# A streaming-encoder step on one core: front pieces spread over the expert half blocks in other proportions, and attention scores issued ahead of the turn

## The reference

```
z   = RMSNorm(x) @ w_in                  # q, k, v of two attentions, forget logits, gates
p   = softmax(q_m k_m / 8 + bias), m=0,1;  a = (p_0 - lam p_1) @ v        # 8 heads, diff attention
ob  = softmax(q k / 8 + C[t] - C[s]) @ v                                 # 8 heads, FoX
x   = x + (sig(gA) * (norm(oa) @ w_pa) + sig(gB) * (ob @ w_pb)) @ w_o
q   = xb @ wq (xb = RMSNorm(x));  sc = q . subkeys;  top 16 of each half, top 16 of the sums
x   = x + sum over 8 heads x 16 experts of  g * gelu(u_e . xb) * v_e      # rows u_e, v_e gathered
y   = RMSNorm_final(x)
```

## Time and profile before

| | before |
|---|---|
| time, median of 3 runs (lowest to highest) | 2603.12 us (2593.22 to 2603.57) |
| the profiled execution: its time / its span | 2613.62 us / 2611.8 us |
| PE busy | 2156.7 us, 83% of the span |
| DVE busy | 1436.7 us, 55% |
| ACT busy | 524.9 us, 20% |
| mean DMA rate | 293 GB/s |
| mean granted PE clock | 0.867 of full |

### The profile page before, as it was taken

One profiled execution on the slowest core, in us unless ns is written; L12 is line 12 of the kernel. 1 busy time (PEld: TensorE's weight loads), 2 busy tenths in 40 slices (PEclk: granted clock), 3 DMA queues, 4 the chain that ended last, 5 costly groups with the idle time before them and its releaser, 6 DMA issues. The chain is left out here.

```text
span 2611.8 us, 23600 instructions
## 1 busy us (share of the span) xinstructions
PE 2156.7 (83%) x7844; PEld 1226.7 (47%) x7844; DVE 1436.7 (55%) x3495; ACT 524.9 (20%) x1354; POOL 693.0 (27%) x697
## 2 busy tenths in 40 slices
PE   7989989989488986887997778989875998998775
PEld 6845566556245642344663234466321434664321
DVE  0021113666355369667559865554894656337956
ACT  2321101111152111343110134301111432011111
POOL 0000000244122123233233522332443223123433
PEclk9988899999679997898998877899887777778778
DMA  8832355698768896788999966699989558888887
GB/s 250 280 106 71 123 190 181 243 394 302 300 236 310 338 350 256 295 309 328 404 405 368 354 258 237 244 402 403 415 323 389 214 222 303 329 305 323 320 324 313
DMA packets 139305, 765.05 MB, mean 293 GB/s; under 512 B 18608, under 2 KB 42464, under 8 KB 52016
## 3 DMA queue, kind: packets, MB, share of 16 engines
q0 software_dynamic: 78336, 570.46, 56.1%
q1 hardware_dynamic: 24912, 154.73, 16.2%
q10 hardware_dynamic: 35936, 38.35, 4.4%
HBM read 744.77 MB, written 18.30 MB: 292 GB/s over the span
## 5 line engine op out<-in xcount | busy, mean ns | idle before, releaser
L1187 PE MATMUL acc<-ring,diag 128*128 128x512 f32 (+1 forms) x1720 | 947.8, 704 | 244.6 <-DVE diag L1521 237.0
L597 POOL DMA_INDIRECT ring<-in_uv,stage x544 | 634.8, 1167 | 1386.8 <-issue 843.2
L1510 DVE CUSTOM_DVE_ANT_0 ring<-ring,xb 128x1024 f32<-128x1024 f32 x544 | 649.5, 1220 | 139.3 <-DMA ring<-in_uv,stage 129.0
L1187 PEld LDWEIGHTS acc<-ring,diag 128*128 128x128 f32 (+1 forms) x1720 | 361.5, 221 | 751.6 <-issue 425.3
L869 ACT ACTIVATE gel<-dots 128x1 f32<-128x1 f32 x544 | 105.5, 201 | 1001.8 <-DVE dots L1510 983.7
L1521 DVE TENSOR_SCALAR diag<-ident,gel,gw 128x128 f32<-128x128 f32 x406 | 141.5, 357 | 216.3 <-ACT gel L869 204.3
L967 PE MATMUL pz<-F,wbuf 128*128 128x416 f32 (+1 forms) x656 | 242.8, 530 | 3.6 <-issue 1.4
L615 POOL COPY stage<-idx 128x4 int32<-128x4 int32 x136 | 55.4, 408 | 508.0 <-DVE gw L1466 488.7
L967 PEld LDWEIGHTS pz<-F,wbuf 128*128 128x128 f32 (+1 forms) x656 | 126.7, 196 | 113.1 <-issue 113.1
L1366 DVE TENSOR_REDUCE nmax<-ps 128x1 f32<-128x128 f32 (+4 forms) x72 | 35.6, 495 | 241.3 <-PE ps L1026 83.7
L1535 DVE SCALAR_TENSOR_TENSOR vsum<-ring,coefd,vsum 128x1024 f32<-128x1024 f32 x109 | 140.7, 1291 | 4.5 <-DVE coefd L1528 0.7
(11 more groups left out here) (267 smaller groups left out, 1997.6 us busy)
## 6 DMA issues: line engine op xcount, KB each, us to landing
wbuf<-in_w_z SPq DMA_DIRECT2D x52, 1024.0 KB, 5.4
wbuf<-in_w_q SPq DMA_DIRECT2D x40, 1024.0 KB, 8.1
wbuf<-in_w_pa SPq DMA_DIRECT2D x20, 1024.0 KB, 7.5
wbuf<-in_w_o SPq DMA_DIRECT2D x20, 1024.0 KB, 7.8
wbuf<-in_w_pb SPq DMA_DIRECT2D x20, 512.0 KB, 6.8
ring<-in_uv,stage POOLq DMA_INDIRECT x544, 8.4
zT<-F ACTq DMA_DIRECT2D x28, 208.0 KB, 2.9
wbuf<-in_w_sk SPq DMA_DIRECT2D x5, 1024.0 KB, 7.0
```

Of the source, the lines that this page charges most:

```text
L597: pool.indirect_dma_start(out=ring[:, slot, :], out_offset=None, in_=d["uv"], in_offset=bass.IndirectOffsetOnAxis(ap=stage[:, a, k:k + 1], ...
L1187: last = nc.tensor.matmul(acc[0:nq, c * 512:(c + 1) * 512], diag[:, parity, 0:nq], ring[:, slot, D + c * 512:D + (c + 1) * 512], start=Fal ...
L1510: nc.vector.tensor_tensor_reduce(out=u, in0=u, in1=xb[:, t % 2, :], scale=1.0, scalar=0.0, op0=ALU.mult, op1=ALU.add, accum_out=dots[:, sl ...
```

## The change

It has three parts. The prices in `weight_of` are others, so the same pieces fall behind other half blocks. The scores of a head are issued one step earlier on PE (for fronts 0 to 3; front 4 keeps its step, but the scores come ahead of the turn), and on ACT and DVE the exponential and the maximum of head s come ahead of the copy and the merge of head s-1. Front 0 gets four score banks, the two halves of `acc` being the third and fourth, and the projections of every front rotate over four banks.

```
-    if what == "project":
-        return 12.0
+    if what == "project":
+        return 1.4
     if p == 0:
-        return 12.0 if i == TILES - 1 else 4.0
+        return 3.0 if i == TILES - 1 else 0.5
     if ATTEND <= p < NORM_O:
-        return 5.0
+        return 1.8
     if p >= TOP:
-        return 6.0
+        return 1.8
+    if YPROJ <= p < OPROJ:
+        return 0.7
     if OPROJ <= p < NORM_X or QPROJ <= p < SCORE:
-        return 1.8
-    return 4.0 if p in (NORM_O, TURN_O, NORM_X, TURN_X) else 3.5
+        return 0.45
+    return 0.5
...
+        def banks(t):
+            return ps + ([acc[:, 0:512], acc[:, 512:1024]] if t == 0 else pz)
...
         def score_banks(t):
-            return 4 if 0 < t < TILES - 1 else 2
+            return 4 if t < TILES - 1 else 2
...
+                ahead = score_banks(t) == 4
+                if step_ == 0 and ahead:
+                    for v in STEPS[0]:
+                        for n in score_tasks(v):
+                            scores(n)
+                coming = step_ + ahead
+                for v in STEPS[coming] if coming < len(STEPS) else []:
+                    for n in score_tasks(v):
+                        scores(n)
                 before = STEPS[step_ - 1] if 1 <= step_ <= len(STEPS) else []
-                now = STEPS[step_] if step_ < len(STEPS) else []
-                for i in range(max(len(before), len(now))):
-                    if i < len(before):
-                        turn(before[i])
-                    if i < len(now):
-                        for n in score_tasks(now[i]):
-                            scores(n)
-                    if i < len(before):
-                        pv(before[i], i == 1)
+                for i in range(len(before)):
+                    turn(before[i])
+                    pv(before[i], i == 1)
...
-                        if f >= 2:
-                            pe.wait_ge(pq_stored, PC * t + f - 1)
+                        if f >= 4:
+                            pe.wait_ge(pq_stored, PC * t + f - 3)
                         for k in range(8):
-                            last = nc.tensor.matmul(ps[f % 2][:, 0:nq], w[:, k, j * P:(j + 1) * P],
+                            last = nc.tensor.matmul(banks(t)[f % 4][:, 0:nq], w[:, k, j * P:(j + 1) * P],
```

More of the change, by code:

```diff
@@ L768, in attend @@
                 nq, nk = rows_of(t), keys_of(t)
+                for v in STEPS[s] if s < len(STEPS) else ():
+                    for n in score_tasks(v):
+                        act.wait_ge(maxed, 24 * t + n + 1)
+                        if n >= 4:
+                            m = n - 4
+                            act.wait_ge(turned, 16 * t + (m // 2 if m < 16 else m - 8) + 1)
+                        nc.scalar.activation(fa(t).prob[0:nq, n % 4, 0:nk], score_bank(t, n)[0:nq, 0:nk], ACT.Exp,
+                                             bias=nmax[0:nq, n:n + 1], accum_out=rsum[0:nq, n:n + 1]
+                                             ).then_inc(exped, 1)
                 for u in STEPS[s - 1] if 1 <= s <= len(STEPS) else ():
@@ L844, in front @@
                         act.wait_ge(pq_mm, PC * t + f + 1)
-                        nc.scalar.activation(fa(t).pqT[:, f, 0:nq], ps[f % 2][:, 0:nq], ACT.Copy).then_inc(pq_stored, 1)
+                        nc.scalar.activation(fa(t).pqT[:, f, 0:nq], banks(t)[f % 4][:, 0:nq], ACT.Copy).then_inc(pq_stored, 1)
                 elif p == SCORE:
@@ L849, in front @@
                         nc.scalar.activation(fa(t).sc[0:nq, 4 * q:4 * q + 4, :],
-                                             ps[q % 2][0:nq, 0:512].rearrange("p (k q) -> p k q", k=4), ACT.Copy
+                                             banks(t)[q][0:nq, 0:512].rearrange("p (k q) -> p k q", k=4), ACT.Copy
                                              ).then_inc(sc_stored, 1)
@@ L1114, in front @@
                         for k in range(4):
-                            last = nc.tensor.matmul(ps[f % 2][:, P:P + nq], wb[:, k, j * P:(j + 1) * P],
+                            last = nc.tensor.matmul(banks(t)[f % 4][:, P:P + nq], wb[:, k, j * P:(j + 1) * P],
                                                     fa(t).obT[:, k, 0:nq], start=(k == 0), stop=(k == 3))
@@ L1342, in attend @@
                     open_attention(t)
+                for v in STEPS[s] if s < len(STEPS) else ():
+                    for n in score_tasks(v):
+                        dve.wait_ge(scored, 24 * t + n + 1)
+                        nc.vector.tensor_reduce(nmax[0:nq, n:n + 1], score_bank(t, n)[0:nq, 0:nk], AX.X, ALU.max,
+                                                negate=True).then_inc(maxed, 1)
                 for u in STEPS[s - 1] if 1 <= s <= len(STEPS) else ():
@@ L1375, in merge @@
                     dve.wait_ge(y_mm, 8 * t + f + 1)
-                    step(nc.vector.tensor_tensor(fa(t).mT[:, f, 0:nq], ps[f % 2][:, 0:nq], fa(t).gates[:, f, 0:nq], ALU.mult))
-                    step(nc.vector.tensor_tensor(fa(t).ybg[:, 0:nq], ps[f % 2][:, P:P + nq], fa(t).gates[:, 8 + f, 0:nq],
+                    step(nc.vector.tensor_tensor(fa(t).mT[:, f, 0:nq], banks(t)[f % 4][:, 0:nq], fa(t).gates[:, f, 0:nq], ALU.mult))
+                    step(nc.vector.tensor_tensor(fa(t).ybg[:, 0:nq], banks(t)[f % 4][:, P:P + nq], fa(t).gates[:, 8 + f, 0:nq],
                                                  ALU.mult))
@@ L1386, in add_x @@
                 cc = slice(c * CW, (c + 1) * CW)
-                nc.vector.tensor_tensor(x2[0:nq, cc], ps[c % 2][0:nq, 0:CW], fa(t).xres[0:nq, cc], ALU.add
+                nc.vector.tensor_tensor(x2[0:nq, cc], banks(t)[c][0:nq, 0:CW], fa(t).xres[0:nq, cc], ALU.add
                                         ).then_inc(x2_stored, 1)
```

33 lines of the change are left out of this document (9 added, 24 removed).

## The result

The changed kernel takes 2656.88 us (median of 4 runs, 2645.55 to 2665.97), the kernel before 2601.65 us on the same chip (4 runs). The ratio is 1.0217, with a 95% interval of 1.0169 to 1.0264: **some 55 us slower**, where 31 us faster was forecast, and outside the range.

A forecast was written before the change was run, and what follows sets the result against it. Beside attention nothing was full, PE and DVE taking turns; beside projections PE and DMAs were full, beside the search DVE. Terms -8 + 4 - 9.5 - 12 - 5, say -31, gave 2583 us profiled, 2572 us median; range 2518 to 2614.

The forecast's parts named there:

- Front 0, -8: Front 0, ahead of the experts: 10.5 us of merge waits go, 4 us of copy waits come, free banks save 2.
- Tile 0, +4: Tile 0: chunks -10, attention +8, projections -6 and search +12 us, in sum 4 us longer.
- 135 against 126.9: Tile 0's attention: 21 half blocks instead of 13 take 135 us, 112 of DVE work and 23 of idle time.
- Tile 1, -9.5: Tile 1: attention +1.5, norm -4 and projections -7 us, in sum 9.5 us shorter.
- tile 2, -12: Tile 2: attention -1 us at clock 0.87, the rest as in tile 1, in sum 12 us shorter.
- I take 0.96: Tile 1's attention: PE's clock rises from 0.88 to 0.96 as most idle pieces go, giving 159.5 us.
- The first step also stands directly behind the load … I add 4: Tile 1's attention: the first step, directly behind the load of the queries, adds 4 us of idle time.
- Tile 3, -5: Tile 3: front 4's attention +6 us and its projections -11 us, in sum 5 us shorter.
- Projections ... -11: Tile 3, front 4's projections: ten half blocks instead of 14 at the same clock 0.73 save 11 us.
- (B): Rival: filled gaps bring the clock back in attention, up to -85 us, 2518 to 2555 us; chance 0.22.
- (D): Rival: 26 moved half blocks cost their transfer beside attention, as adds held back delay gathers; +24, 2627 us; chance 0.12.
- (E): Rival: a drain at each table load delays ACT's copy by 1.4 us, giving 2642 us; chance 0.03.

The follow-up runs named there:

- order_only: The changed kernel with the old prices, keeping the new order and banks: 2589.74 us, ratio 0.9973 to the kernel before.
- load_apart: The changed kernel with the load of the queries of fronts 1 to 3 priced 2.0 instead of 0.5: 2624.57 us, ratio 1.0120.
- load_23: The changed kernel with the load of the queries priced 2.0 instead of 0.5 for fronts 2 and 3 only: 2615.48 us, ratio 1.0066.
- chunks_back: order_only with new prices for front 1 alone (load 2.0), tile 0's chunks standing where they were before: 2593.51 us, ratio 0.9971.
- wide_order: front4_old with front 4's y and query projections 128 columns wide instead of 32: 2538.51 us, ratio 0.9764.
- wide_234: wide_order with the new prices for fronts 2 to 4 (load 2.0): 2536.34 us, ratio 0.9750.
- load_tight: order_only with the load of the queries of fronts 2 and 3 priced 1.0 instead of 4.0: 2605.09 us, ratio 1.0026.
- front4_old: order_only with front 4's attention in the old order on PE, ACT and DVE: 2577.25 us, ratio 0.9897.
- prices_3: order_only with the new prices for front 4 alone: 2595.39 us, ratio 0.9993.

## Why the prediction was wrong

Three steps carry the miss. A half block was priced by the work of the busy engine, where tile 0 shows 3.9 us each outside the chunks. The load directly ahead of the first step was priced at 4 us, where it costs 10 to 13 us a tile. And the clock was taken to rise or to stay, where it was 0.84 and 0.82 in attention and fell to 0.69 beside front 4's projections. The rest of this section takes them one by one.

**Where the loss lies.** By the ratios, over order_only: new prices in tile 0 +19 us, in fronts 2 and 3 +1, for front 4 +5. The sum, 25, is to be held against load_apart, which has all of them: +38, give or take 12. The medians come closer (33.8 and 34.8), but each difference carries about 10 us of uncertainty, so the costs add up within it and no more. The load beside the first step is the rest of the change, 25 us over load_apart (39 over load_23). Against that stand the 7 us of the order. Only the tile 0 part and the load part are clear of the noise.

**Work was right, idle time and clock were not.** The sum had 133, 144 and 126.5 us of work at full clock for the attention of tiles 1, 2 and 3; busy time by clock gives 156.79 x 0.84 = 132, 174.55 x 0.82 = 143 and 163.76 x 0.77 = 126. The steps that failed:

- *Front 0, -8.* Measured -0.5: the first dot moved from 498.8 to 498.3 us. In the 14 kernels with the new order it lies from 491.9 to 504.1 us, 498.7 on average, so nothing was gained. The merge waits of 10.5 us went, waits for the copy (6.0 us, 15 of them) and for the first exponential (2.9 us) came. "0.3 us a step" was 0.4, the wait for the exponential was not in the sum, and the 2 us from free banks did not show.
- *Tile 0, +4.* Measured +13.4, and +26 against the same order with old prices (540 us). The +12 of the search came (84.3 to 96.3 us). Chunks and attention together were right by luck: "170 us for hb 0 to 11" was 155.5 and "135 against 126.9" was 147.6, so 303.1 us where 305 was said, and two errors of 13 to 15 us cancel. In attention PE idled 34.5 us instead of the 23 that the step took over from the old stretch (15.6 us of it at the queries, where it was 11.3), at a clock of 0.72 instead of 0.78. The "-6" of the projections was 0 (123.9 us), and the two stretches that the sum left out grew by 3 us each (12.0 to 14.9, 24.9 to 27.7). What the sum did not see is that the order alone takes 13 us off this tile and the new places put 26 on it: a half block that left the chunks saved 1.6 us there and cost 3.9 us elsewhere, as chunks_back shows; the step priced it by DVE's work alone.
- *Tile 1, -9.5, and tile 2, -12.* Measured +7.8 and -7.4. Attention of tile 1 was to take 159.5 us and took 185.9. Two steps failed. The larger in the trace is the clock: "I take 0.96" was 0.84, which is 18 of the 26 us, and in tile 2 "0.87" was 0.82. The other is "**The first step also stands directly behind the load … I add 4**". It took the transfer's latency as the price, and left out that the adds of half block 0 wait behind the whole first step, now two heads of scores, and the gathers behind the adds. load_23 shows about 13 us a tile in its trace for it (10 on average over the kernels of either kind), and in its tile 1 the clock is 0.87, so part of the clock's loss belongs to this step. The rest of the tiles was -20 and -22 us, more than the -11 said, mostly because the stretch of NORM_O and TURN_O has one half block in it and not two (22.7 to 10.5 us, where -4 was said).
- *Tile 3, -5.* Measured +20.3. Attention "at 0.76" was at 0.77, but "idle 23.7 - 3" was 38.1: front 4's new order is no gain of 3 us but a loss, 17 us more of waits for merge and copy. "Projections ... -11": 14 half blocks took 150.0 us, and the next, beside the first search piece, 14.0; now 11 with that piece in them take 167.2. Four half blocks fewer, and 3 us more. The text named the danger ("it may as well fall further: at 0.65 the term is 0") and took the old 0.73; it was 0.69. The clock is one part of the miss. The other is that the saving was too large even with the clock held, 2.5 us between wide_order and wide_234: the work left, and idle time came in its place.

**The rivals.** (B) rested on gaps being the cause of the low clock; its rule, in the Trainium skill (TensorE: Matmul & The Clock Gate, What's actually happening), is that activity releases the throttle. The share of time in which PE is busy did not tell the clock here: 91% went with 0.69 and 89% with 0.92 in the same stretch. Nor did filling the gaps bring attention to full clock. Before it was 0.88 in tile 1 and 0.79 in tile 2, and in order_only, with the same half blocks, it is 0.84 and 0.82. The same code in tile 1 has 0.84 to 0.91 in four traces, so a change of 0.04 is scatter, but none comes near 1. (D) named the ring and the adds held behind the scores, but took it for a cost of each of 26 half blocks; it is the cost of the first step of tiles 1 and 2. Its other half, that a half block costs some 4 us beside attention, is near what tile 0 shows (3.9). (E), 2642 us, came nearest in time, but its cause is not there. In after the copy is followed directly by the load:

```profile
1123.41 0.49 ACT L794 ACTIVATE F<-pt 128x384 f32<-128x384 f32 x1 [0.51 <-PE pt L1050]
1123.92 1.28 ACT L875 ACT_TABLE_LOAD   x1
1125.21 0.34 ACT L875 ACTIVATE gel<-dots 128x1 f32<-128x1 f32 x2
```

The drain of 1380 ns that the Trainium skill (ScalarE: Activation LUTs, What ACT_TABLE_LOAD costs) adds to each switch has no room between 1123.90 and 1123.92, nor between the load's end and 1125.21.

**What stays open**: how much of the difference between load_tight and load_23 is real; the 14 us between load_apart and load_23; what part of the order's gain is due to the banks; why the clock in the attention of tiles 1 and 2 stays at 0.91 or less; and the part of tile 2's difference that is scatter, since kernels with the same plan there (order_only, chunks_back, front4_old, prices_3) take 456 to 468 us.

## What to carry to other kernels

Price the move of a block at both ends from a stretch where one can be added or taken away, not from the busy engine's work: here it was 1.6 us where PE is full anyway and 3.9 us elsewhere. When two pieces fall into one slot, look at what is held back behind the second: a wait of 5 us for a transfer, with two heads of scores behind it, stopped the gathers for 28 us instead of 12. Issuing scores a step ahead moved PE's waits more than it removed them; with four banks it was worth about 1% at best (front4_old, 0.9897), and the same order without the distance added waits.

## What the hardware showed

Widening front 4's matmuls from 32 to 128 columns, with three quarters of the result thrown away, shortened the stretch from 167.2 to 129.1 us, since the granted clock rose from 0.69 to 0.92. By the ratios it is worth 42 us on the changed kernel (1.0217 to 1.0056) and 35 us on the version with the old prices (0.9897 to 0.9764), more than all of the reordering.
